# A fused transformer block on one core: the next expert pair's tokens gathered by slot instead of by column block

## The reference

```
for each of 32 experts e:   y += ((silu(h @ w_gate[e]) * (h @ w_up[e])) * cw[:, e]) @ w_down[e]
h = rmsnorm(x, g) * (1 + sc) + sh        # 256 x 2048
w_gate[e], w_up[e]: 2048 x 512           w_down[e]: 512 x 2048
cw[t, e]: non-zero for the two experts that token t is routed to
```

## Time and profile before

| | us |
|---|---|
| time, median of 3 runs | 1552.59 (1552.22 to 1553.93) |
| the profiled execution's own time | 1551.45 |
| its span, first to last instruction | 1549.6 |
| TensorE busy in it | 1509.9 (97%) |
| VectorE busy | 714.8 (46%) |
| ScalarE busy | 289.9 (19%) |
| data moved by DMA | 589.96 MB |

### The profile page before, as it was taken

How to read it: one execution, slowest core, us unless ns; L and a number is a source line. 1 busy time by engine, 2 the same in 40 slices (tenths; PEclk the granted TensorE clock), 3 DMA queues, 4 the chain that set the end, 5 groups by cost and what they waited for, 6 DMA issues and landing times.

```text
span 1549.6 us, 19402 instructions
## 1 busy us (share of the span) xinstructions
PE 1509.9 (97%) x7980; PEld 811.3 (52%) x7980; DVE 714.8 (46%) x1289; ACT 289.9 (19%) x520; POOL 39.8 (3%) x57
## 2 busy tenths in 40 slices
PE   5999999999999999999999999999999999999996
PEld 2888888855654446344344444434434434434432
DVE  3574767676887636243233333332332332432325
ACT  2100311121332303111111112112012112112113
POOL 1001000000001200000000000000000000000003
PEclk9999999999999999999999999999999999999998
DMA  9999777799878996999999999999999999999994
GB/s 363 396 385 367 265 261 283 268 360 353 319 277 314 363 411 250 401 405 425 429 428 427 430 429 427 430 429 427 428 429 428 429 428 428 428 429 428 428 429 194
DMA packets 102802, 589.96 MB, mean 381 GB/s; under 512 B 6224, under 2 KB 16944, under 8 KB 77408
## 3 DMA queue, kind: packets, MB, share of 16 engines
q1 hardware_dynamic: 100384, 580.93, 92.4%
q0 software_dynamic: 1696, 5.66, 1.1%
q10 hardware_dynamic: 672, 2.66, 0.4%
HBM read 587.07 MB, written 2.16 MB: 380 GB/s over the span
## 4 chain that ended last, share of the span: by engine, by line
PE 82%; DMA 14%; DVE 2%; issue 0%; ACTq 0%; SPq 0%; ACT 0%; DVEq 0%
PE bank L1092 24%; DMA ring<-in_w_up 12%; PE bank L1203 11%; PE bank L930 7%; PE bank L646 7%; PE bank L1064 6%; PE bank L680 5%; PE bank L1084 5%; PE bank L871 4%; DMA ring<-in_w_ada 2%; PE bank L714 2%; PE bank L693 1%; PE bank L696 1%; DMA ring<-in_w_in 1%; PE bank L1100 1%; PE bank L837 1%
## 5 line engine op out<-in xcount | busy, mean ns | idle before, releaser
L1092 PE MATMUL bank<-ring,RN 128*64 128x512 f32 x1520 | 333.8, 593 | 3.7 <-DMA ring<-in_w_up 3.6
L1092 PEld LDWEIGHTS bank<-ring,RN 128*64 128x64 f32 x1520 | 108.4, 137 | 221.4 <-issue 208.7
L1203 PE MATMUL bank<-ring,RN 128*64 128x512 f32 x992 | 219.7, 595 | 1.0 <-issue 1.0
L1203 PEld LDWEIGHTS bank<-ring,RN 128*64 128x64 f32 x992 | 68.9, 137 | 137.8 <-issue 136.0
L2219 DVE COPY RG<-bank 64x512 f32<-64x512 f32 x64 | 44.1, 689 | 194.9 <-PE bank L1203 187.2
L1064 PEld LDWEIGHTS bank<-RN,RX 128*128 128x128 f32 x976 | 111.5, 192 | 13.0 <-issue 13.0
L1064 PE MATMUL bank<-RN,RX 128*128 128x128 f32 x976 | 115.7, 277 | 0.0
L930 PE MATMUL bank<-ring,RT 128*128 128x512 f32 x256 | 113.0, 596 | 0.8 <-DVE RT L2000 0.8
L1084 PE MATMUL bank<-RG,RN 128*128 128x512 f32 x240 | 109.5, 599 | 0.0
L2149 DVE TENSOR_SCALAR RN<-bank,aff 128x128 f32<-128x128 f32 x256 | 87.3, 403 | 47.6 <-PE bank L1064 45.7
L2205 DVE TENSOR_TENSOR RN<-bank,RN 128x512 f32<-128x512 f32 x32 | 22.1, 691 | 179.5 <-PE bank L1092 179.5
(11 more groups left out here) (387 smaller groups left out, 1488.0 us busy)
## 6 DMA issues: line engine op xcount, KB each, us to landing
ring<-in_w_down SPq DMA_DIRECT2D x64, 2048.0 KB, 15.5
ring<-in_w_up SPq DMA_DIRECT2D x63, 2048.0 KB, 21.0
ring<-in_w_ada SPq DMA_DIRECT2D x32, 2048.0 KB, 10.8
ring<-in_w_gate SPq DMA_DIRECT2D x32, 2048.0 KB, 19.7
ring<-in_w_in SPq DMA_DIRECT2D x18, 2048.0 KB, 9.3
RH<-in_w_gate SPq DMA_DIRECT2D x16, 2048.0 KB, 21.8
RT<-in_w_gate SPq DMA_DIRECT2D x16, 2048.0 KB, 18.9
ring<-in_w_ada SPq DMA_DIRECT2D x48, 512.0 KB, 11.7
```

Of the source, the lines that this page charges most:

```text
L1092: last = mm(bank[n // 2][c:c + CAP, :], tokT[:, k, q * CAP:(q + 1) * CAP], w[:, i, :], start=k < 2, stop=k >= KT - 2, skip_group_check=True)
L1203: last = mm(bank[2 + n % 2][64 * (n // 2):64 * (n // 2) + 64, :], hidT[:, k * CAP:(k + 1) * CAP], wdn[:, n * BLK:(n + 1) * BLK], start=k = ...
```

## The change

The gather inside `pair` is made in two steps. `gather_rows(p, m)`: the one-hot table is the weights and 512 features of `x_t` move, two matmuls for each m (one for each token tile), which leaves slots on the partitions in bank 4 + m. ACT copies the bank to a buffer of 128 x 512 in SBUF, `slot_rows`, one buffer for all four m (`slots_in`). `gathered_T(p, m)`: four transpositions turn it to features x slots, in banks 4, 5, 6 and 4. DVE's `tokens` reads these as before, all four after `hidT` now. The gather of the first pair stays as it was. `slot_rows` is put behind the constants in `cst`; `mod` gets smaller.

```diff
@@ -217,14 +217,14 @@
         RT = sb("RT", [P, 32, 256])
         RN = sb("RN", [P, 5120])
         RG = sb("RG", [P, 2, D])
-        cst = sb("cst", [P, C_COLS])
+        cst = sb("cst", [P, C_SUM + BLK])
         vec = sb("vec", [P, 2, P])
         vrow = RN[:, 0:256].rearrange("p (a b) -> p a b", a=2)
         wide = sb("wide", [P, 2 * BLK])
         part = wide[:, 0:BLK]
         head_sums = [wide[:, :], RN[:, 3584:4608]]
         silv = sb("silv", [P, KT])
-        mod = sb("mod", [P, 6 * KT])
+        mod = sb("mod", [P, 2 * KT])
         ones = sb("ones", [P, P])
         st = sb("st", [P, 64])
         gts = sb("gts", [P, TT, N_GATES])
@@ -292,6 +292,7 @@
         hid = RN[:, 2304:2816]
         sil = RN[:, 2816:3328]
         hidT = RN[:, 3328:3584]
+        slot_rows = cst[:, C_SUM:C_SUM + BLK]
         ohw = RN[:, 3584:3840].rearrange("p (t s) -> p t s", t=TT)
         ohwT = RN[:, 3840:4096]
         rows = RG[:, 0, :]
@@ -303,6 +304,8 @@
         AHEAD = blocks_of(RT[:, KT:2 * KT, :].rearrange("p a b -> p (a b)"))
         dhid, dsil, dhidT = hid, sil, RN[:, 0:512]
         GB = [4, 5, 6]
+        FIRST_BANK = GB + GB[0:1]
+        ROWS_BANK, TOKEN_BANK = [4, 5, 6, 7], [4, 5, 6, 4]
         posi = RG[:, 0, 3 * S:4 * S].bitcast(I32)
         sin_angle, cos_angle = RG[:, 0, 4 * S:5 * S], RG[:, 0, 5 * S:6 * S]
 
@@ -1053,16 +1056,30 @@
             keep_clock(8, 7)
 
 
-            def gather_part(n, m):
-
-                if m >= 3:
-                    pe.wait_ge(sig("gathered_used").sem, (n - 1) * 4 + 1)
-                elif not isinstance(n, int):
-                    pe.wait_ge(sig("gathered_used").sem, (n - 1) * 4)
-                for k in range(4 * m, 4 * m + 4):
+            def gather_last_part():
+
+                wait(pe, "gathered_used", 1)
+                for k in range(12, 16):
                     for tt in range(TT):
-                        last = mm(bank[GB[m % 3]][:, (k % 4) * P:(k % 4 + 1) * P], x_t[:, tt, k * P:(k + 1) * P],
+                        last = mm(bank[GB[0]][:, (k % 4) * P:(k % 4 + 1) * P], x_t[:, tt, k * P:(k + 1) * P],
                                   onehot[:, tt, :], start=tt == 0, stop=tt == TT - 1)
+                last.then_inc(sig("gathered").sem, 1)
+
+            def gather_rows(p, m):
+
+                if m == 3:
+                    pe.wait_ge(sig("ohwT_copied").sem, p + 1)
+                for tt in range(TT):
+                    last = mm(bank[ROWS_BANK[m]][:, :], onehot[:, tt, :], x_t[:, tt, m * BLK:(m + 1) * BLK], start=tt == 0, stop=tt == TT - 1)
+                last.then_inc(sig("rows_gathered").sem, 1)
+
+            def gathered_T(p, m):
+
+                pe.wait_ge(sig("rows_in_slots").sem, p * 4 + (m + 1))
+                if m == 3:
+                    pe.wait_ge(sig("gathered_used").sem, p * 4 + 5)
+                for j in range(4):
+                    last = tr(bank[TOKEN_BANK[m]][:, j * P:(j + 1) * P], slot_rows[:, j * P:(j + 1) * P], ident)
                 last.then_inc(sig("gathered").sem, 1)
 
             pe.wait_ge(sig("onehot").sem, 1)
@@ -1169,7 +1186,7 @@
                                 pe.wait_ge(sig("gathered_used").sem, p * 4 + (2 * n + m + 1))
                             row_blocks(n, q, w, range(4 * m, 4 * m + 4))
                         if n == 0 and first:
-                            gather_part(1, 3)
+                            gather_last_part()
                         if n == 1 and first:
                             wait(pe, "over_counted")
                             inc(mm(bank[7][:, 192:193], ones[:, :], rt[:, 200:201], start=True, stop=True), "over_sum")
@@ -1179,19 +1196,21 @@
                         pe.wait_ge(sig("scatter_added").sem, p * 8)
                     if q == 1:
                         pe.wait_ge(sig("onehot").sem, p + 2)
-                        for m in range(3):
-                            gather_part(p + 2, m)
-                    if q == 1:
+                        for m in range(2):
+                            gather_rows(p, m)
                         pe.wait_ge(sig("ohw").sem, p + 1)
                         for tt in range(TT):
                             last = tr(bank[7][:, tt * P:(tt + 1) * P], ohw[:, tt, :], ident)
                         last.then_inc(sig("ohwT").sem, 1)
+                        gather_rows(p, 2)
                     pe.wait_ge(sig("hidden").sem, e + 1)
                     hidden_T()
                     if q == 0 and scatter_last:
                         scatter(p, range(6, 8))
                     if q == 1:
-                        gather_part(p + 2, 3)
+                        gathered_T(p, 0)
+                        gather_rows(p, 3)
+                        gathered_T(p, 1)
 
                     pe.wait_ge(sig("rows_copied").sem, e * 2 + 2)
                     pe.wait_ge(sig("hiddenT_copied").sem, e + 1)
@@ -1204,6 +1223,8 @@
                                       wdn[:, n * BLK:(n + 1) * BLK], start=k == 0, stop=k == 3, skip_group_check=True)
                         if k % 2 == 1:
                             last.then_inc(sig("expert_used").sem, 1)
+                            if q == 1:
+                                gathered_T(p, 2 + k // 2)
 
             pair(0, True, False)
             with pe.Fori(1, NE // 2 - 1) as p:
@@ -1510,6 +1531,13 @@
 
             act.sem_inc(sig("rows_copied").sem, 1)
 
+            def slots_in(p, m):
+
+                act.wait_ge(sig("rows_gathered").sem, p * 4 + (m + 1))
+                if m:
+                    act.wait_ge(sig("gathered").sem, p * 4 + (m + 4))
+                fn(slot_rows, bank[ROWS_BANK[m]][:, :], ACT.Copy).then_inc(sig("rows_in_slots").sem, 1)
+
             def expert_act(p, q, last=False):
 
                 e = p * 2 + q
@@ -1518,12 +1546,17 @@
                 act.wait_ge(sig("gate_sum").sem, e + 1)
                 fn(sil[0:64, :], hid[0:64, :], ACT.Silu)
                 fn(sil[64:128, :], hid[0:64, :], ACT.Silu).then_inc(sig("silu").sem, 1)
+                if q == 1 and not last:
+                    slots_in(p, 0)
                 if q == 1:
                     act.wait_ge(sig("ohwT").sem, p + 1)
                     fn(ohwT, bank[7][:, 0:S], ACT.Copy).then_inc(sig("ohwT_copied").sem, 1)
                 act.wait_ge(sig("hiddenT").sem, e + 1)
                 fn(sil[:, 0:4 * CAP].rearrange("p (f s) -> p f s", f=4), bank[0][:, :].rearrange("p (f s) -> p f s", f=4)[:, :, CAP:P],
                    ACT.Copy).then_inc(sig("half_copied").sem, 1)
+                if q == 1 and not last:
+                    for m in range(1, 4):
+                        slots_in(p, m)
                 act.wait_ge(sig("expert_used").sem, e * HB + (5 if last else 6))
                 for n in range(2):
                     ins = fn(rows[64 * q:64 * q + 64, n * 1024:n * 1024 + BLK], bank[2][64 * n:64 * n + 64, :], ACT.Copy)
@@ -2205,15 +2238,13 @@
                     tt_op(hid[:, :], bank[1][:, :], sil[:, :], ALU.mult).then_inc(sig("hidden").sem, 1)
                     if q == 0 and scatter_last:
                         add_scattered(p, range(6), first)
-                    if q == 1 and gather_next:
-                        tokens(p + 2, range(3))
                     dve.wait_ge(sig("half_copied").sem, e + 1)
                     parts = [w.rearrange("p (f s) -> p f s", f=4) for w in (hidT, bank[0][:, :], sil[:, 0:4 * CAP])]
                     tt_op(parts[0], parts[1][:, :, 0:CAP], parts[2], ALU.add).then_inc(sig("hiddenT_copied").sem, 1)
                     if q == 0 and scatter_last:
                         add_scattered(p, range(6, 8), first)
                     if q == 1 and gather_next:
-                        tokens(p + 2, range(3, 4))
+                        tokens(p + 2, range(4), TOKEN_BANK)
                     dve.wait_ge(sig("expert_used").sem, e * HB + 6)
                     for n in range(2):
                         ins = v.tensor_copy(rows[64 * q:64 * q + 64, n * 1024 + BLK:(n + 1) * 1024], bank[3][64 * n:64 * n + 64, :])
```

More of the change, by code:

```diff
@@ L1267, in _ @@
                 act.dma_start(vrow[r0:r0 + a[name].shape[0], 0, :], a[name]).then_inc(sig("vectors0_in").sem, 16)
-            act.dma_start(cst[:, :], a["consts"]).then_inc(sig("consts_in").sem, 16)
+            act.dma_start(cst[:, 0:C_COLS], a["consts"]).then_inc(sig("consts_in").sem, 16)
             for tt in range(TT):
@@ L2142, in onehot_pair, with tokens @@
                 last.then_inc(sig("onehot").sem, 1)
-            def tokens(n, ms=range(4)):
+            def tokens(n, ms, banks):
                 for m in ms:
@@ L2148, in tokens @@
                     for k in range(4 * m, 4 * m + 4):
-                        ins = ts(tokT[:, k, :], bank[GB[m % 3]][:, (k % 4) * P:(k % 4 + 1) * P], aff[:, 2, k:k + 1], aff[:, 3, k:k + 1],
+                        ins = ts(tokT[:, k, :], bank[banks[m]][:, (k % 4) * P:(k % 4 + 1) * P], aff[:, 2, k:k + 1], aff[:, 3, k:k + 1],
                                  ALU.mult, ALU.add)
```

(4 more changed lines are left out.)

## The result

The changed kernel takes 1576.76 us (1576.24 to 1577.99), the kernel before 1552.40 (four runs of each): a ratio of 1.0159, 95% interval 1.0146 to 1.0171. That is 24.4 us slower; forecast was +27.3 us, 1580, with 1571 to 1591 as range. The profiled execution has a span of 1574.3 us, before 1549.6: 24.7 more.

What follows compares the result with a forecast made beforehand. Experts' stage: weights by DMA at 58.74 us a pair, TensorE at 57.08, nearly level. Per pair -0.28 + 1.79 + 0.66 = +2.17; 15 x 2.17 = 32.6, less 5.3 of waits: +27.3 us, 1580, range 1571 to 1591.

Steps and rivals of the forecast that it cites:

- TensorE and DMA nearly level, 5.3 us between them: Experts' stage: weights arrive at 58.74 us a pair, TensorE needs 57.08; its waits for weights, 5.3 us, can hide added work.
- The removed gather and the rows by slot: Gather in each pair: 64 instructions removed, 7.16 us, and 16 of 512 columns added, 6.88: net -0.28 us.
- 16 turns at 0.112: Gather in each pair: 16 added transpositions on TensorE at 0.112 us each, 1.79 us (1.7 to 1.92).
- Two visits to the other shape, 0.66: Third and fourth transposition groups, at the 128*64 down projection: two steps in and out, 2 x 0.33 us a pair.
- No new wait exposed: Gather's hand-overs between TensorE, ACT and DVE: all covered by other work, so +2.17 us a pair stands.
- The tightest place: Transposition group 1 waiting for ACT's copy 1: ready at 7.5, wanted at 8.2, 0.7 us of room, covered by rows 3.
- The sum: Whole kernel: 15 pairs x 2.17 = 32.6 us, less 5.3 of waits for weights, +27.3 us.
- 1, the DMA holds the end: Experts' stage: the DMA's pace hides added work under 0.35 us a pair; time 1552.6; chance 0.05.
- 2, faster: Gather: transpositions lie beneath other work at no cost, leaving -0.28 us a pair; 1550.4 or 1548.4; chance 0.02.
- 3, the turns cost their duration of 0.273: Gather: each transposition costs its whole duration, 4.37 us for 16, 4.75 a pair, +66 us: 1619; chance 0.02.
- the Trainium skill's sentence on transposes and the clock gate: TensorE: transpose mode does not count as activity for the clock gate; the forecast saw no fall and charged nothing.
- 4, the exposed buffer: Single slot buffer: ACT answers later, TensorE stands; one turn-about of 1.0 us a pair, +15 us: 1595; chance 0.10.

Runs made afterwards that it cites:

- experiment 7: The kernel before with half of one of the six 2 MB pieces of the experts' weights not loaded: 1546.24 us, ratio 0.9970.
- experiment 6: The kernel before with 16 transpositions of a constant added in each pair, ahead of the two of ohw: 1572.21 us, ratio 1.0130.
- experiment 5: The kernel before with 3 transpositions of a constant added in each pair, ahead of the two of ohw: 1551.93 us, ratio 1.0001.
- experiment 3: The changed kernel with three slot buffers and all 16 transpositions a pair ahead of the down projection: 1568.37 us, ratio 1.0103.
- experiment 2: The changed kernel with two slot buffers and the last two groups of transpositions both after the down projection: 1572.42 us, ratio 1.0131.
- experiment 1: The changed kernel with its 16 transpositions a pair left out, rows by slot, ACT copies and waits kept: 1551.79 us, ratio 0.9996.
- experiment 4: The changed kernel, single slot buffer, with rows 3 gathered before the hidden transpositions, so nothing stands between transposition groups 0 and 1: 1590.60 us, ratio 1.0247.
- experiment 8: The changed kernel with half of one of the six 2 MB pieces of the experts' weights not loaded: 1576.82 us, ratio 1.0161.

## Why the prediction was right

- **TensorE and DMA nearly level, 5.3 us between them.** Right. The medians alone (5.4 in experiment 7, 5.8 in experiment 6, 5.0 hidden in experiment 5) leave up to 2.6 us either way. The traces are sharper, from the first gather's start to the last down projection's: 1522.37 - 658.11 = 864.26 us in the kernel before, 1517.01 - 658.12 = 858.89 with lighter weights (experiment 7), so 5.4 of waits; 1544.41 - 659.33 = 885.08 with 26.25 of added work (experiment 6), so 5.4 hidden; 1547.71 - 657.88 = 889.83 in the changed kernel with 15 x 2.06 = 30.9 added, so 5.3 hidden.
- **The removed gather and the rows by slot,** forecast -0.28 a pair. Measured 7.07 against 7.34, -0.27.
- **16 turns at 0.112,** 1.79. Measured 4 x 0.44 = 1.76 in groups, 1.78 in one run of 16 (experiment 3).
- **Two visits to the other shape, 0.66.** Right in kind (experiment 2), a little too large: 2 x (0.59 - 0.44) + 0.14 + 0.15 = 0.59. The step in is 0.15 when transpositions follow, where the row used (0.18) was of matmuls. This and the turns (1.76, not 1.79) are the 0.1 us by which 2.17 missed 2.06 to 2.08.
- **No new wait exposed.** Right: neither the changed kernel's chain nor that of experiment 1 has a gap at the gather. The tightest place had the room that was forecast, 0.7 us. Its hand-over from ACT to TensorE, taken as 0.2 from a hand-over between ACT and DVE, was 0.05 in experiment 4, and the turn-about cost 0.92 there, not 1.0.
- **The sum.** 15 x 2.06 = 30.9, less 5.3, is 25.6; the span grew by 24.7, where 27.3 was forecast. So 1.7 of the 2.6 us too many lie in the pair, and 0.9 in two places that were not counted. One is the end: the last scatter used to start 1530.48 - 1522.37 = 8.11 us after the start of the last down projection in the kernel before, and now starts 1555.11 - 1547.71 = 7.40 after it, 0.71 less. The rows are these, of the kernel before and then of the changed one:

```profile
1522.37 7.13 PE L1125 MATMUL bank<-ring,RN 128*64 128x512 f32 x32 [0.31 <-issue]
1530.48 7.11 PE L1141 MATMUL bank<-RG,RN 128*128 128x512 f32 x16 [0.97 <-issue]
```

```profile
1547.71 7.09 PE L1142 MATMUL bank<-ring,RN 128*64 128x512 f32 x32 [0.31 <-issue]
1555.11 7.11 PE L1158 MATMUL bank<-RG,RN 128*128 128x512 f32 x16 [0.31 <-issue]
```

The kernel before has one wait there that the list of waits puts down to the weights, and the changed kernel has none:

```profile
PEld bank L1125 <- DMA ring<-in_w_down: 0.7, 1, 0.7
```

But this wait of a load is not the 0.71: the down projection itself takes 7.13 us with it and 7.09 without. The rest is TensorE's idle time behind it, 0.97 us and 0.31, for which the profile names no releaser. With lighter weights (experiment 7) the kernel before has no such idle time, and its last scatter starts 7.11 us after the down projection:

```profile
1517.01 7.09 PE L1126 MATMUL bank<-ring,RN 128*64 128x512 f32 x32 [0.31 <-issue]
1524.12 7.11 PE L1142 MATMUL bank<-RG,RN 128*128 128x512 f32 x16
```

The idle time is also long in experiments 1 and 5, where TensorE waits for weights too (1.14 and 1.28), and between nothing and 0.47 in the other runs. So it goes with weights that come late; by what way stays open. The other place is the start: the first gather begins 0.23 us earlier, at 657.88 and not 658.11. That is chance: the profiles of all ten kernels have it between 657.84 and 660.16. 30.9 - 5.3 - 0.7 - 0.2 = 24.7, then, but only the first two terms are explained.

**The rivals.** 1, the DMA holds the end: it would have done so with up to 0.35 us a pair, as experiment 5 shows with 0.33; the change adds six times that. 2, faster: excluded by the result; and in experiment 1 even freed TensorE time bought nothing that can be told from noise (-0.7 us, -2.0 to +0.8). 3, the turns cost their duration of 0.273: refuted by 0.111 in a run of 16 and 0.11 in groups of 4. As for the Trainium skill's sentence on transposes and the clock gate (TensorE: Matmul & The Clock Gate, Part 4): with 16 more turns a pair the granted clock of the slices stayed where it was, and the price of turns held at every place, so no run here shows an effect of it. 4, the exposed buffer: real when its cover is removed, 0.92 us a pair, absent here.

No arrangement of the turns that was tried comes down to the kernel before. The best, experiment 3, still adds 15 x (1.78 - 0.27) = 22.7 us of TensorE work where 5 to 6 are free. And the gather's own gain of 0.27 us a pair, even without any turns, is worth nothing under the DMA's floor (experiment 1). So no version here that loads all the weights beats the kernel before.

## What to carry to other kernels

Where two resources are nearly level, first measure how many microseconds of the bound engine's time the other one still hides, then hold the added work against that number; a saving on the side that waits is worth nothing. Wider matmuls that need a transposition behind them pay only if the weight loads they save exceed the turns: here 0.27 us saved, 1.76 spent. Work of another array shape put into a stream costs at each visit, so gather such work in one place, and look for buffers that allow it.

## What was not expected of the hardware

- A transposition beside 128*64 matmuls costs a group of four 0.15 us on the way in and the neighbour 0.15 on the way out; it was expected at 0.18 and 0.15.
- The DMA fell idle without cost. The forecast had its rate at 425 GB/s throughout. In the changed kernel the DMA's view of the stretch from 1085 to 1145 us (40 slices of 1.5 us) shows it empty twice, from some 1097 and 1111 us, about where SP's written order of refills changes (`IN_ORDER`, expert 16; that this is the cause was not tried); TensorE did not wait, and with lighter weights (experiment 8) the time was the same.

```profile
GB/s 415 382 426 437 393 448 404 273 11 0 186 393 470 382 470 404 470 22 0 76 240 382 459 415 448 426 415 459 382 492 360 513 360 492 382 470 393 459 415 415
```
